# Trading PSUM banks between the gated units and the merge units, turning the last S5 outputs two jobs later, and fetching the residual rows tile by tile in a hybrid decoder trunk

## The chip, the core and the metric

One core of a Trainium2 chip runs the whole program. The metric is the device time of one launch in microseconds (us). The engines are TensorE (PE, matmuls), VectorE (DVE), ScalarE (ACT), GpSimd (POOL) and SyncE (SP, here only DMA issues); each runs its own instruction list in order and waits on semaphores.

## The reference

Two layers over 528 tokens (16 meta tokens and 512) of width 1024. Each layer mixes tokens in two parallel branches and then runs a channel mixer (dense in layer 0, top-2-of-8 experts in layer 1).

```python
z = hn @ w_in[layer]                      # 3584 columns: u_s5, x_lru, g_lru, gates
gates = sigmoid(z[..., o_m:] + merge_bias).reshape(bsz, t, 2, D_MODEL)
# S5 branch: state space model per group, GELU, then a gated unit
y = gelu(y_ssm); y_a = (y * sigmoid(y @ w_glu + b_glu)) @ s5_w_proj
y_b = rglru_branch(...) @ lru_w_proj
y = gates[:, :, 0, :] * y_a + gates[:, :, 1, :] * y_b
hs = hs + y @ w_out[layer]
hn = rmsnorm(hs, ffn_norm[layer])         # then the channel mixer
```

## The kernel before

Activations lie transposed, channels on partitions in tiles of 128, and tokens along the free dimension: `hs`, `hn`, `gates`, `xh` and so on have one row block `[:, m, :]` for each channel tile m. Every fp32 operand of a large product is split into a high and a low part (`xh`, `xl` for activations, `wh`, `wl` for weights), and a product is three matmuls: high by high, high by low, low by high. In layer 0 each runs as two matmuls of 264 tokens, in layer 1 mostly as one of 512.

The weights come in **units** of 8 blocks of 128x128 (512 KB). SP fetches unit u into `raw` when the low part of unit u-3 has been made; ACT makes `wh` (`split_hi`, L740) and DVE `wl` (`split_lo`) two units ahead of PE's use. `unit` (L1724) runs a unit as 8 **jobs**, one for each block, of three products. A dictionary `between` can put other work ahead of job n of a unit.

A mixer has 28 input units k (`U_IN`), 2 gated units (`U_GLU`), 8 merge units and 8 output units. Beside the input units run the S5 steps of 8 batches of groups, in the four `side` banks.

- **Input unit 27** is the last. Ahead of its job 1 stands `turn_last` (L1712): PE transposes the last S5 outputs `ys`, which ACT copied out of PSUM (L849, in `s5_last`). ACT copies the result into `zt` (L852). Ahead of job 4 stands `regroup_last` (L1720), 8 products that place `zt` by channels into `side` banks 2 and 3. ACT applies the GELU to the half that came by DMA (L855) and to this half (L857), and rounds it into `y1h` (L860); DVE makes `y1l`. Only after `s5_last` does ACT run its last step for unit 27, a sigmoid that reads unit 27's sums in `acc` (L904) and frees them.
- **Gated units** g = 0, 1 multiply `y1h`/`y1l` by the GLU weights. `glu_sums` puts g = 0 into both pairs of `acc` banks and g = 1 into the `side` banks. PE waits, ahead of g = 0, until ACT has freed both halves of `acc` (`free(0, a1)`, `free(1, a1)`). ACT takes the sigmoid of the sums (L945).
- **Merge units** m = 0 to 7 compute both branches' projections for channel tile m. `merge_sums` puts even m into `acc`, odd m into `side`. DVE multiplies the sums by `gates[:, m, :]` and `gates[:, 8 + m, :]`, adds, and signals `mg_ready`; ACT rounds to `xh` (L954), and DVE makes `xl`. The gates occupy the memory of `hs` and `hn`, tile by tile.
- After the eight merge steps ACT issues eight DMAs (L957) that bring the residual rows `hs[:, m, :]` back from HBM (from the input `xT` in layer 0, from `hs_d` in layer 1). Then come the square-root table and the next weight splits.
- **Output units** m = 0 to 7 multiply by `w_out`, in `acc[:, m % 2]`. DVE waits for all eight row blocks (`hs_back`) before it adds the first one (L1372); a no-op behind each add frees that half of `acc` (L1375). Output unit 2 needs the half that unit 0 used. From unit 2 on, PE adds sums of squares for the norm (L1750) in `side` bank 0.

## Time and profile before

| what | value |
|---|---|
| three timed runs | 1754.74, 1755.19, 1757.77 us; median 1755.19 |
| span of the profiled execution | 1751.1 us |
| median less span | 4.1 us |
| PE busy | 1646.0 us, 94% |
| DVE, ACT, POOL busy | 58%, 44%, 21% |
| chain that ended last | PE 78%, DVE 7%, issue 5% |

The span runs from the first to the last instruction of one profiled execution; its other overheads lie around it and no time of its own is given beside the span, so the sums of the prediction are made against 1751.1 and the 4.1 us to the median are carried over unchanged. In the rows below a matmul's own duration (0.28 us for 264 columns) is longer than the distance from one to the next, since matmuls overlap.

### The profile page before, as it was taken

Reading aid. Unit: us, or ns where it says so; the run is one execution under the profiler, and the core shown is the slowest. Engines: PE = TensorE matmul, PEld = TensorE weight load, DVE = VectorE, ACT = ScalarE, POOL = GpSimd, SP = SyncE. Lnnn points to the kernel's source line nnn. Section 1 sums busy time; section 2 is a strip of 40 time slices with the busy share of each in tenths; the row PEclk is TensorE's granted clock in tenths of the full one; section 3 lists DMA queues with packets and bytes.
Section 4 is the critical chain, followed back from the end, with each engine's and each line's share of the span. In section 5 each row is a group of like instructions: output and inputs, shape, how many; then the busy total and the mean of one; then the engine's idle time right before and its main releaser. Section 6 shows DMA issues by size and latency. Waiting matters only on the chain.

```text
span 1751.1 us, 26958 instructions
## 1 busy us (share of the span) xinstructions
PE 1646.0 (94%) x10652; PEld 1465.3 (84%) x10652; DVE 1020.8 (58%) x1286; ACT 777.5 (44%) x947; POOL 370.7 (21%) x662
## 2 busy tenths in 40 slices
PE   6899999989999999998999999979999999999992
PEld 5799989989999999998987877757788777777872
DVE  6868567443333233324766766368556766865985
ACT  4354463332221222323453563247536655755772
POOL 7688630020000000004777700020000000000001
PEclk9899999999999999998999999999999999999996
DMA  4523222473232222224523224059658967966994
GB/s 161 118 83 92 77 79 86 146 273 123 85 96 85 87 94 91 89 85 148 119 81 94 73 87 146 25 231 405 242 189 286 358 220 242 384 247 227 368 370 158
DMA packets 99444, 291.24 MB, mean 166 GB/s; under 512 B 27376, under 2 KB 27504, under 8 KB 99200
## 3 DMA queue, kind: packets, MB, share of 16 engines
q1 hardware_dynamic: 84624, 245.43, 41.3%
q0 software_dynamic: 9504, 33.60, 5.4%
q10 hardware_dynamic: 5200, 10.64, 1.8%
q8 instruction: 75, 1.23, 0.3%
q14 instruction: 41, 0.34, 0.1%
HBM read 261.39 MB, written 28.24 MB: 165 GB/s over the span
## 4 chain that ended last, share of the span: by engine, by line
PE 78%; DVE 7%; issue 5%; POOL 4%; DMA 3%; ACT 3%; ACTq 0%; POOLq 0%; DVEq 0%; SPq 0%
PE acc L1740 41%; PE acc L2005 7%; PE acc L2006 7%; PE acc L2007 7%; PE side L1740 3%; PE acc L1783 2%; PE acc L2003 2%; DMA mraw<-in_W 2%; PE acc L2004 2%; DVE rot L1154 1%; POOL pt L533 1%; PE side L1803 1%; PE side L2051 1%; POOL pt L649 1%; PE side L1865 1%
## 5 line engine op out<-in xcount | busy, mean ns | idle before, releaser
L1154 DVE TENSOR_TENSOR mwl<-mraw,mwh 128x1024 fp32r<-128x1024 f32 x288 | 337.7, 1220 | 75.2 <-ACT mwh L1049 74.4
L1740 PE MATMUL acc<-xh,wh 128*128 128x264 f32 (+1 forms) x1584 | 374.9, 306 | 5.0 <-DVE xl L1154 1.8
L1740 PE MATMUL acc<-xl,wh 128*128 128x264 f32 (+1 forms) x1584 | 367.0, 302 | 0.0
L1740 PE MATMUL acc<-xh,wl 128*128 128x264 f32 (+1 forms) x1584 | 366.1, 301 | 0.0
L1154 DVE TENSOR_TENSOR wl<-raw,wh 128x1024 fp32r<-128x1024 f32 x164 | 203.5, 1242 | 212.4 <-ACT wh L740 211.7
L1049 ACT ACTIVATE mwh<-mraw 128x1024 fp32r<-128x1024 f32 x288 | 288.1, 1053 | 61.5 <-PE acc L2007 31.8
L1740 PEld LDWEIGHTS acc<-xh,wh 128*128 128x128 f32 x1584 | 255.5, 189 | 19.8 <-issue 3.3
L1740 PEld LDWEIGHTS acc<-xh,wl 128*128 128x128 f32 x1584 | 253.9, 189 | 9.6
L1740 PEld LDWEIGHTS acc<-xl,wh 128*128 128x128 f32 x1584 | 254.3, 189 | 9.0
L740 ACT ACTIVATE wh<-raw 128x1024 fp32r<-128x1024 f32 x164 | 172.2, 1051 | 143.7 <-PE acc L1740 141.1
L2005 PE MATMUL acc<-mwh,xth 128*128 128x512 f32 x432 | 171.1, 396 | 7.9 <-ACT ytok L1115 5.4
L2007 PE MATMUL acc<-mwl,xth 128*128 128x512 f32 x432 | 169.1, 391 | 0.0
L2006 PE MATMUL acc<-mwh,xtl 128*128 128x512 f32 x432 | 169.1, 391 | 0.0
L697 POOL DMA_DIRECT2D yg_d<-ytok x11 | 6.0, 541 | 524.3 <-ACT ytok L1115 520.7
L2005 PEld LDWEIGHTS acc<-mwh,xth 128*128 128x128 f32 x432 | 81.5, 189 | 27.7 <-DVE mwl L1154 6.7
L2007 PEld LDWEIGHTS acc<-mwl,xth 128*128 128x128 f32 x432 | 81.5, 189 | 17.4
L2006 PEld LDWEIGHTS acc<-mwh,xtl 128*128 128x128 f32 x432 | 81.5, 189 | 16.4
L597 POOL DMA_DIRECT2D gw<-in_wg x2 | 1.1, 546 | 424.7 <-DVE hs L1408 424.7
L2005 PE MATMUL acc<-mwh,hth 128*128 128x512 f32 x216 | 86.0, 398 | 0.0
L2007 PE MATMUL acc<-mwl,hth 128*128 128x512 f32 x216 | 84.2, 390 | 0.0
L2006 PE MATMUL acc<-mwh,htl 128*128 128x512 f32 x216 | 84.2, 390 | 0.0
L1740 PE MATMUL acc<-fh,wh 128*128 128x264 f32 x384 | 78.8, 286 | 0.0
(405 smaller groups left out, 2626.1 us busy)
## 6 DMA issues: line engine op xcount, KB each, us to landing
mraw<-in_W SPq DMA_DIRECT2D x288, 512.0 KB, 5.3
raw<-in_W SPq DMA_DIRECT2D x164, 512.0 KB, 3.5
xg_d<-zero POOLq DMA_DIRECT2D x15, 512.0 KB, 9.9
yg_d<-ytok POOLq DMA_DIRECT2D x9, 512.0 KB, 4.7
xt<-xg_d POOLq DMA_DIRECT2D x8, 512.0 KB, 8.5
pbuf<-in_s5m POOLq DMA_DIRECT2D x16, 192.0 KB, 3.2
yg_d<-zero POOLq DMA_DIRECT2D x5, 512.0 KB, 20.8
hs<-in_xT SPq DMA_DIRECT2D x8, 264.0 KB, 8.1
```

The source lines that it names most:

```text
L533: link(g.tensor_tensor(out, a, b, op))
L649: g.tensor_tensor(z1, phase[:, :, :, 0:n], br, ALU.mult)
L740: a.activation(wh[s][:, :], raw[s][:, :], ACT.Copy).then_inc(hi_ready[s], 1)
L1049: a.activation(mwh[w][:, :], mraw[j % RAWS][:, :], ACT.Copy).then_inc(wide_hi, 1)
L1154: return v.tensor_tensor(out, a, b, op)
L1740: ins = mm(out, w, x[:, t0:t1], start=first and i == 0, stop=last and i == 2)
L1783: ins = mm(acc[:, a, b, 0:TH], w, x[:, b * TH:(b + 1) * TH], start=k == 0 and i == 0, stop=k == DK - 1 and i == 2)
L2003: ins = mm(out[0:HALF], hi[:, 0:HALF], mwl[w][:, cols], start=False, stop=False)
L2004: return ins if first else mm(out, hi, mwh[w][:, cols], start=False, stop=last)
L2005: mm(out, hi, mwh[w][:, cols], start=first, stop=False)
L2006: mm(out, lo, mwh[w][:, cols], start=False, stop=False)
L2007: return mm(out, hi, mwl[w][:, cols], start=False, stop=last)
```

## The change

Four edits, in both layers.

1. The gated unit g = 0 and the even merge units take the `side` banks, the gated unit g = 1 and the odd merge units take `acc`. The semaphores that free the banks are traded with them. Ahead of gated unit 0 PE now waits for the last GELU (`y1_ready`, which ACT's L857 completes, the last reader of `side`), and ahead of gated unit 1 for ACT's sigmoids of units 26 and 27.
2. Output unit 0 writes `side` banks 0 and 1; output units 1 to 7 stay in `acc`.
3. In unit 27 `turn_last` stands ahead of job 3 instead of job 1, and `regroup_last` ahead of job 5 instead of job 4.
4. ACT issues the DMA of residual row block m behind the rounding of merge step m, instead of all eight after step 7.

```diff
         def glu_sums(g, i):
-            return side[:, 2 * i:2 * i + 2, :] if g else acc[:, i, :, :]
+            return acc[:, i, :, :] if g else side[:, 2 * i:2 * i + 2, :]
         def merge_sums(m):
-            return (side[:, 0:2, :], side[:, 2:4, :]) if m % 2 else (acc[:, 0, :, :], acc[:, 1, :, :])
+            return (acc[:, 0, :, :], acc[:, 1, :, :]) if m % 2 else (side[:, 0:2, :], side[:, 2:4, :])
+        def out_sums(m):
+            return acc[:, m % 2, :, :] if m else side[:, 0:2, :]
...
                     a.activation(xh[:, m, AT0[l]:T], ft[:, 0, AT0[l]:T], ACT.Copy).then_inc(xh_ready, 1)
-
-                for m in range(DK):
                     act.dma_start(hs[:, m, :], (hs_d if l else xT)[:, m, :]).then_inc(hs_back, 16)
+
                 sqrt_table()
...
-                    v.tensor_tensor(live(l, hs[:, m, :]), live(l, hs[:, m, :]), summed(l, acc[:, m % 2, :, :]),
+                    v.tensor_tensor(live(l, hs[:, m, :]), live(l, hs[:, m, :]), summed(l, out_sums(m)),
...
-                         between={1: lambda: turn_last(l), 4: lambda: regroup_last(l)} if k == U_IN - 1 else None)
+                         between={3: lambda: turn_last(l), 5: lambda: regroup_last(l)} if k == U_IN - 1 else None)
...
                 for g in range(U_GLU):
                     if g == 0:
+                        pe.wait_ge(y1_ready, (l + 1) * (MT + 1))
+                    else:
                         free(0, a1)
                         free(1, a1)
...
-                        if m % 2 == 0:
+                        if m % 2:
                             free(i, a0 + 15 + m // 2)
                         else:
                             pe.wait_ge(side_free[i], l * SIDE_MIX + 1 + m // 2)
...
                 for m in range(DK):
-                    free(m % 2, a0 + 19 + m // 2)
                     if m == 0:
+                        pe.wait_ge(side_free[0], (l + 1) * SIDE_MIX)
                         pe.wait_ge(xl_ready, xl_mix_end(l) - 1)
+                    else:
+                        free(m % 2, a0 + 19 + m // 2)
```

PE in input unit 27 of layer 0, before. `wh_57` and `wl_60` are the high and low weights of the ring slot of unit 27; three rows are one job. The transposes are L1712, the products that regroup are L1720.

```order
L1740 MATMUL acc<-xh,wl_60 128x264 x2
L1712 MATMUL side<-ident,ys 66x128 x4
L1740 MATMUL acc<-xh,wh_57 128x264 x2
L1740 MATMUL acc<-xl,wh_57 128x264 x2
L1740 MATMUL acc<-xh,wl_60 128x264 x2
L1740 MATMUL acc<-xh,wh_57 128x264 x2
L1740 MATMUL acc<-xl,wh_57 128x264 x2
L1740 MATMUL acc<-xh,wl_60 128x264 x2
L1740 MATMUL acc<-xh,wh_57 128x264 x2
L1740 MATMUL acc<-xl,wh_57 128x264 x2
L1740 MATMUL acc<-xh,wl_60 128x264 x2
L1720 MATMUL side<-ident,zt 64x66 x8
```

The same place after the change, from the end of job 1 on (lines have moved by three).

```order
L1743 MATMUL acc<-xh,wl_60 128x264 x2
L1743 MATMUL acc<-xh,wh_57 128x264 x2
L1743 MATMUL acc<-xl,wh_57 128x264 x2
L1743 MATMUL acc<-xh,wl_60 128x264 x2
L1715 MATMUL side<-ident,ys 66x128 x4
L1743 MATMUL acc<-xh,wh_57 128x264 x2
L1743 MATMUL acc<-xl,wh_57 128x264 x2
L1743 MATMUL acc<-xh,wl_60 128x264 x2
L1743 MATMUL acc<-xh,wh_57 128x264 x2
L1743 MATMUL acc<-xl,wh_57 128x264 x2
L1743 MATMUL acc<-xh,wl_60 128x264 x2
L1723 MATMUL side<-ident,zt 64x66 x8
```

Three jobs stand ahead of the transposes instead of one, two jobs between them and the regrouping instead of three, and three jobs behind it instead of four.

ACT at the end of the merge in layer 0, before: the steps for merge units 5, 6 and 7 and the way to output unit 0.

```order
L954 ACTIVATE xh<-ft 128x528
L740 ACTIVATE wh_59<-raw_56 128x1024
L954 ACTIVATE xh<-ft 128x528
L740 ACTIVATE wh_57<-raw_54 128x1024
L954 ACTIVATE xh<-ft 128x528
L957 DMA hs<-in_xT 128x528 x8
L755 ACT_TABLE_LOAD
L755 ACTIVATE warm<-ones 128x1
L740 ACTIVATE wh_58<-raw_55 128x1024
```

The same stretch of ACT after the change.

```order
L958 ACTIVATE xh<-ft 128x528
L959 DMA hs<-in_xT 128x528
L744 ACTIVATE wh_59<-raw_56 128x1024
L958 ACTIVATE xh<-ft 128x528
L959 DMA hs<-in_xT 128x528
L744 ACTIVATE wh_57<-raw_54 128x1024
L958 ACTIVATE xh<-ft 128x528
L959 DMA hs<-in_xT 128x528
L759 ACT_TABLE_LOAD
L759 ACTIVATE warm<-ones 128x1
L744 ACTIVATE wh_58<-raw_55 128x1024
```

Each merge step has one of the eight issues behind its rounding, and one is left ahead of the table load.

## Rows read from the trace of the kernel before

**Rows 1.** The page: shares of the chain that ended last, by engine.

```profile
PE 78%; DVE 7%; issue 5%; POOL 4%; DMA 3%; ACT 3%; ACTq 0%; POOLq 0%; DVEq 0%; SPq 0%
```

**Rows 2.** Chain of waits, layer 0, unit 27 and gated units: start, us, what.

```profile
243.98 0.29 ACT ys L849
...
244.94 2.19 PE acc L1740 x18
247.13 1.08 PE side L1720 x16
248.21 3.12 PE acc L1740 x24
251.32 1.81 issue
253.13 6.08 PE acc L1740 x48
259.22 5.84 PE side L1740 x48
```

**Rows 3.** Timeline of PE in unit 27, layer 0 (start, us, operation, idle before).

```profile
242.40 0.40 PE L1740 MATMUL acc<-xh,wl 128*128 128x264 f32 x2
244.31 0.63 PE L1712 MATMUL side<-ident,ys 128*66 128x128 f32 x4 [1.51 <-ACT ys L849]
```

**Rows 4.** Timeline of ACT beside it.

```profile
244.98 0.59 ACT L852 ACTIVATE zt<-side 66x512 f32<-66x512 f32 x1 [0.72 <-PE side L1712]
...
246.88 0.64 ACT L855 ACTIVATE yt<-yt 64x528 f32<-64x528 f32 x1
248.25 0.61 ACT L857 ACTIVATE yt<-side 64x528 f32<-64x528 f32 x1 [0.72 <-PE side L1720]
...
252.33 0.70 ACT L904 ACTIVATE gates<-acc,cols 128x528 f32<-128x528 f32 x1
```

**Rows 5.** Timeline of DVE beside it: low parts of gated unit 0's weights, last tile.

```profile
242.00 1.23 DVE L1154 TENSOR_TENSOR wl<-raw,wh 128x1024 fp32r<-128x1024 f32 x1 [2.02 <-ACT wh L740]
...
250.10 1.17 DVE L1154 TENSOR_TENSOR y1l<-yt,y1h 128x528 fp32r<-128x528 f32 x1 [3.75 <-ACT y1h L860]
```

**Rows 6.** Chain of waits, layer 1, the same place.

```profile
1016.51 0.29 ACT ys L849
...
1016.84 0.63 PE side L1712 x4
...
1020.65 2.97 PE acc L1740 x12
1023.62 1.92 issue
...
1031.33 5.56 PE side L1740 x24
```

**Rows 7.** Timeline of PE in layer 1: last matmul of unit 27's job 0.

```profile
1015.43 0.40 PE L1740 MATMUL acc<-xh,wl 128*128 128x512 f32 x1
```

**Rows 8.** Timeline of ACT's DMA issues, layer 0, after merge step 7.

```profile
314.23 0.65 ACT L954 ACTIVATE xh<-ft 128x528 fp32r<-128x528 f32 x1 [4.28 <-DVE ft L1154]
314.24 3.84 ACTq L957 DMA_DIRECT2D hs<-in_xT  x8
```

**Rows 9.** Chain of waits, layer 0, output units 0 to 2.

```profile
317.50 5.51 DMA hs<-in_xT
...
323.11 0.72 DVE hs L1372
```

**Rows 10.** Timeline of PE, first matmuls of output unit 2, layer 0.

```profile
323.93 0.51 PE L1740 MATMUL acc<-xh,wh 128*128 128x264 f32 x2 [0.16 <-DVEq L1375]
```

**Rows 11.** Timeline of PE, layer 1: end of output unit 1, start of unit 2.

```profile
1092.13 0.39 PE L1740 MATMUL acc<-xh,wl 128*128 128x512 f32 x1
1094.08 0.50 PE L1740 MATMUL acc<-xh,wh 128*128 128x512 f32 x1 [1.56 <-DVEq L1375]
```

**Rows 12.** The row fetches of L957 (both layers), by line.

```profile
DMA to landing us min/median/max: 2.8/4.2/6.4
```

**Rows 13.** The weight fetches of L491, by line, whole program.

```profile
DMA to landing us min/median/max: 3.3/3.5/9.3
```

**Rows 14.** Windows: engines' busy us, then PEclk, DMA share, GB/s at the end.

```profile
251.20:253.13 1.93, 0.12 (x2) 0.03 (x1) 1.20 (x2) 1.92 (x3) 0.00 (x0) 1.00 0.00 0
...
324.00:375.00 51.00, 46.34 (x387) 43.72 (x388) 22.56 (x28) 15.01 (x22) 11.48 (x21) 0.93 0.44 148
```

More of the change, by code:

```diff
@@ L945, in mixer @@
                         a.activation(live(l, gt[:, i, :]), summed(l, glu_sums(v, i)), ACT.Sigmoid,
-                                     bias=col("b_glu", l, 2 * v + i)).then_inc((side_free if v else acc_free)[i], 1)
+                                     bias=col("b_glu", l, 2 * v + i)).then_inc((acc_free if v else side_free)[i], 1)
                     for i in range(2):
@@ L1337, in mixer @@
                         m = 2 * g + i
-                        dve.wait_ge(*((side_free[i], l * SIDE_MIX + 1) if g else (acc_free[i], a1 + 1)))
+                        dve.wait_ge(*((acc_free[i], a1 + 1) if g else (side_free[i], l * SIDE_MIX + 1)))
                         if m >= 2:
@@ L1357, in mixer @@
                         dve.wait_ge(xl_ready, xh_at_mix(l) + m)
-                    freed, n = (side_free, l * SIDE_MIX + 1) if m % 2 else (acc_free, a0 + 15)
+                    freed, n = (acc_free, a0 + 15) if m % 2 else (side_free, l * SIDE_MIX + 1)
                     for i in range(2):
@@ L1892, in mixer @@
                 for m in range(DK):
-                    free(m % 2, a0 + 19 + m // 2)
                     if m == 0:
+                        pe.wait_ge(side_free[0], (l + 1) * SIDE_MIX)
                         pe.wait_ge(xl_ready, xl_mix_end(l) - 1)
+                    else:
+                        free(m % 2, a0 + 19 + m // 2)
                     unit(u0 + U_MIX - DK + m,
-                         [(k, m % 2, xh[:, k, :], xl[:, k, :], k == 0, k == DK - 1) for k in range(DK)],
-                         before={DK - 1: (xl_ready, xl_mix_end(l))} if m == 0 else None, short=l)
+                         [(k, 0, xh[:, k, :], xl[:, k, :], k == 0, k == DK - 1) for k in range(DK)],
+                         before={DK - 1: (xl_ready, xl_mix_end(l))} if m == 0 else None, short=l, sums=(out_sums(m),))
                     if m >= 2:
```

## The prediction

> **What bounds the kernel now.** I read the page first, then the chain of waits, then the timelines of PE, ACT and DVE around the places that the change touches. PE holds 78% of the chain that ended last [rows 1], so a microsecond in which PE stands still in a mixer is a microsecond of the whole, unless something later takes it back. The questions are therefore where PE stands still around input unit 27 and the output units, and what would hold it next.
>
> There are three such stops that the edits touch, each met once in each layer.
>
> First, ahead of the transposes of the last S5 outputs PE sits idle for 1.51 us, released by ACT's copy of `ys` [rows 3]. That copy ends at 243.98 + 0.29 = 244.27 [rows 2], whatever PE does in the meantime, because ACT is working through other things; only one job of unit 27 is behind PE by then.
>
> Second, after the last matmul of unit 27 the chain shows 1.81 us of "issue" and gated unit 0 starts at 253.13 [rows 2]. The profile gives this wait no releaser, but one fits: ACT's sigmoid of unit 27 runs from 252.33 for 0.70 us, to 253.03 [rows 4], and it is what frees the half of `acc` that gated unit 0 overwrites. ACT runs it so late because the whole S5 tail (zt, two GELUs, `y1h`) stands ahead of it in ACT's list. The operands of gated unit 0 were there: its low weights by 243.23 and the last `y1l` by 251.27 [rows 5].
>
> Third, output unit 2 waits for the half of `acc` that DVE frees when it has added unit 0, and DVE waits for all eight residual row blocks. In layer 0 the chain goes through a row fetch of 5.51 us and the add at 323.11 [rows 9] and PE idles only 0.16 us [rows 10]; in layer 1 it idles 1.56 us [rows 11].
>
> **The turn moved by two jobs, and gated unit 0 in the side banks.** These have to be summed together, since they share one stretch. A unit of 48 matmuls takes 5.84 us in steady state, a job 0.73 us [rows 2]. In layer 0 job 0 ends at 242.40 + 0.24 = 242.64 [rows 3]. After the change jobs 1 and 2 follow at once, to 244.11. `ys` is there at 244.27 and the transposes start at 244.31 as before: the same time, with two jobs more behind PE. Jobs 3 and 4 run until about 244.94 - 0.24 + 0.08 + 1.46 = 246.24 (the chain counts the last transposes in full, PE resumes some 0.24 before their end, and a change of shape costs 0.08). The regrouping can start at 246.3; `zt` is ready at 244.98 + 0.59 = 245.57 [rows 4], 0.7 us earlier, so two jobs in between are enough. It takes 1.08 us [rows 2]. The last three jobs take 2.2 us and a restart of 0.1, so unit 27 ends at 249.7. It ended at 248.21 + 3.12 = 251.3 less the overlap, 251.2 [rows 2]: 1.5 us earlier, which is two jobs of 0.73.
>
> Gated unit 0 then no longer asks for the sigmoid of unit 27, but for the last GELU. The regrouping is done at 247.4, the first half's GELU at 246.88 + 0.64 = 247.52, so the second runs from 247.5 for 0.61 us, to 248.1 [rows 4]. Even at its old place it would end at 248.86. Unit 27 ends at 249.7, so the new wait has 1.6 us to spare and costs nothing. What is queued behind this wait on PE are only the gated units. The last `y1l`, 0.7 us earlier than before, comes at 250.6 [rows 5] and is needed by job 6 of gated unit 0, at 249.7 + 4.4 = 254.1. The sigmoid of unit 27 is now needed only by gated unit 1, at 249.7 + 5.9 = 255.6; ACT ends it at 252.3 (0.7 us earlier than 253.03). Its cover is 3.3 us; gone, it would be paid one for one. Gated unit 0 starts at 249.7 instead of 253.13: **3.4 us** in layer 0.
>
> In layer 1 a job takes 5.56 / 8 = 0.695 us [rows 6]. Job 0 ends at 1015.66 [rows 7], jobs 1 and 2 at 1017.05, which is 0.25 us later than `ys` (1016.80) [rows 6]; the turn starts at 1017.1 rather than 1016.84. Resuming at 1017.5, two jobs (1.4 + 0.1), the regrouping at 1019.1 (1.08) and three jobs (2.1 + 0.1) put the end of unit 27 at 1022.35. It was 1020.65 + 2.97 = 1023.62, and gated unit 0 began 1.92 us later, at 1025.54 [rows 6]: **3.2 us**.
>
> **The other banks.** The merge units' alternation is turned round as a whole. Each merge unit still writes banks that were read one unit earlier, so the distance stays one unit of 5.84 us; DVE and ACT read from `side` what they read from `acc`, and chain rows give the two the same unit time. Merge unit 0 waits on `side`, freed by sigmoids that are over a whole unit before. Output unit 0 in `side` waits for merge 6's products instead of writing `acc` behind the same products: nothing. Its squares (L1750) go into bank 0 only after DVE's add. I take zero for all of this.
>
> **Residual rows inside the merge.** Eight issues take ACT 3.84 us, 0.48 each [rows 8]. Seven of them move into stretches in which ACT waits 4.28 us for DVE's next sum [rows 8], so they cost ACT nothing on the way; each can hold the next weight split back by up to 0.48 us, and that split serves a unit two units ahead. Behind the rounding of step 7 one issue is left, so the last block is on its way at about 314.6 + 0.45 = 315.1 and lands 2.8 to 6.4 us later [rows 12], at 317.9 to 321.5, where before it was 323.0. The square-root table and the next weight splits come 3.4 us earlier too. Without its stop output unit 2 would start at 323.93 - 0.32 = 323.6 [rows 10], so unit 0 ends one unit earlier, near 317.8, and DVE's add ends between 318.7 and 322.3, before PE asks for it at 323.6. The stop goes: 0.16 us idle and 0.16 of overlap in layer 0 [rows 10], in layer 1 1094.08 - 1092.13 - 0.23 = 1.72 us [rows 11]. In layer 1, with units of 5.56 us, the margin of 1.3 us at the longest landing is some 0.6 us smaller and still positive, so nothing is late next. Sum **2.0 us**.
>
> Total: 3.4 + 3.2 + 2.0 = **8.6 us**. Span 1751.1 - 8.6 = 1742.5; with the 4.1 us around it, **1746.6 us**, 0.49% less. No operation is added or removed, so no other term is needed; what comes behind each mixer starts from PE's or DVE's last step and moves with it as a block.
>
> **The clock, as row and as rule.** In the stop of 1.9 us ahead of gated unit 0 the granted clock stays at 1.00, the 2.4 GHz level [rows 14]. Removing the stop therefore brings nothing on top of its own length. At the end of the mixer of layer 0, where PE idles through the norm, the stretch 324 to 375 has a mean of 0.93 [rows 14]: 0.07 x 51 / 0.5 = 7.1 us at the lower level, 1.2 GHz. The Trainium skill's page "TensorE: Matmul & The Clock Gate", section "Part 1: The HAM clock gate", says that the monitor runs freely and does not reset with the kernel, so where it switches relative to the work depends on phase. By that rule the same joint could lose more or less after a shift; no row here can show it, and it is a rival below.
>
> **Rivals.**
>
> *The joints fall otherwise on the clock.* The change moves everything after layer 0's unit 27 by 3 to 9 us. If the low-clock stretch of 7.1 us is longer or shorter by its half at one joint, 3.6 us of it at half speed are 1.8 us; at two joints in the same direction 3.6. That gives 1743.0 to 1750.2. For it: the three timed runs differ by 3.0 us with nothing changed. Against: a median evens some of it out.
>
> *Only the output part works.* If gated unit 0 still started when it does now, because what ended the 1.81 us was not the sigmoid but something that the profile does not show ("issue" names none), only the 2.0 us and perhaps the two jobs per layer would be saved: if the new stop swallowed the jobs too, 1753.2; that is within 0.2%. Against it stands that the sigmoid's end, 253.03, and PE's start, 253.13, fit to 0.1 us.
>
> *Row fetches in the way of the weights (slower).* Row blocks of 264 KB now travel among weight units of 512 KB. A weight unit is fetched about three units of 5.84 us ahead of its split, some 15 us after ACT's and DVE's own work is taken off, and lands in 3.5 us, 9.3 at the worst [rows 13]. If the rows slowed it beyond 15 us, each of 8 merge units in 2 layers would be late by the excess; at an excess of 1 us that is 16 us less the 8.6, so 1762.6. The decisive point is a landing of 15 us, four times the median. Against: at the end of the merge, where eight row blocks are issued in a row, a row block still lands in at most 6.4 us [rows 12]. The Trainium skill's page "Trainium Kernel Development and Optimization", section "Key Constraints", says that DMAs of all queues share the same 16 engines and interleave, so that a second queue saves only issue time; that is the mechanism, and by it alone 0.78 MB in 5.84 us instead of 0.52 would stretch landings but no total.
>
> **How the numbers follow.** Forecast (7.5 to 9.5 us saved) 0.60; the clock rival (5 to 12 us saved, 0.27; of this about one tenth lies beyond the ends of my range); only a part (0 to 4 us saved) 0.08; slower 0.05. A measurement of this kernel can tell a difference of about 0.2%, 3.5 us, from none: the bound is 1751.7. Faster by more: 0.60 + 0.27 = 0.87. Within: 0.08. Slower: 0.05. The range from 1743.0 to 1751.0 holds the forecast and most of the clock rival and leaves out the last two.
>
> **What the new profile would show.** The transposes of the last outputs start within 0.3 us of their old time after `ys`, with idle of 0.3 us or less in place of 1.51; the products that regroup follow two jobs later without idle; gated unit 0 starts right behind unit 27, about 5.4 us after the transposes in place of 8.8; ACT's sigmoid of unit 27 now runs while gated unit 0 does. Output unit 2 follows unit 1 without a wait on DVE's no-op in both layers, and the landing of the row fetches in the merge is near 3 us. Wrong would be: a wait for the GELU or for `zt` on PE, a longer wait for `wh` or `wl` anywhere in the merge, or a saving that is given back at the norms with a clock of 0.5 for longer than now.

## The result and the profile after

| | before | after |
|---|---|---|
| median (lowest to highest), 4 runs each | 1754.97 us (1753.12 to 1757.77) | 1742.48 us (1739.56 to 1743.21) |
| ratio, 95% interval | | 0.9925 (0.9913 to 0.9936) |
| profiled execution: span | 1751.1 us | 1740.4 us |
| its device time | not known | 1742.03 us |
| mean granted clock in it | 0.979 | 0.977 |

The change saves 12.5 us by the medians, 0.71%; the ratio in the table says 0.75%. The forecast was 8.6 us and 1746.6 us, with a range of 1743.0 to 1751.0: the direction is right, and the time lies 0.5 us below the range. The two profiled spans differ by 10.7 us.

PE in unit 27 and gated unit 0 of layer 0, timeline of after (start, us, operation; an idle time before it would stand in brackets at the end):

```profile
243.78 0.40 PE L1743 MATMUL acc<-xh,wl 128*128 128x264 f32 x2
244.21 0.63 PE L1715 MATMUL side<-ident,ys 128*66 128x128 f32 x4
244.60 0.49 PE L1743 MATMUL acc<-xh,wh 128*128 128x264 f32 x2
...
246.22 1.15 PE L1723 MATMUL side<-ident,zt 66*64 66x66 f32 x16
...
249.36 0.40 PE L1743 MATMUL acc<-xh,wl 128*128 128x264 f32 x2
249.60 0.41 PE L1743 MATMUL side<-y1h,wh 128*128 128x264 f32 x2
```

The idle of 1.51 us ahead of the transposes [rows 3] is gone: jobs 1 and 2 run in it. Gated unit 0 starts at 249.60, 0.24 us behind the last product of unit 27, where it started at 253.13 behind 1.81 us of "issue" [rows 2]. What stood in its way is seen on ACT, timeline of after:

```profile
244.88 0.59 ACT L856 ACTIVATE zt<-side 66x512 f32<-66x512 f32 x1 [0.72 <-PE side L1715]
245.49 1.28 ACT L859 ACT_TABLE_LOAD   x1
...
247.45 0.61 ACT L861 ACTIVATE yt<-side 64x528 f32<-64x528 f32 x1
248.09 1.19 ACT L864 ACTIVATE y1h<-yt 128x528 fp32r<-128x528 f32 x1
...
251.55 0.70 ACT L908 ACTIVATE gates<-acc,cols 128x528 f32<-128x528 f32 x1
...
255.64 1.29 ACT L949 ACTIVATE gt<-side,cols 128x528 f32<-128x528 f32 x2 [2.44 <-PE side L1743]
```

The sigmoid of unit 27 (L908) runs from 251.55, while gated unit 0 is under way: it was 252.33 before [rows 4]. The last GELU (L861), for which PE now waits, is over at 248.06, 1.5 us ahead of the unit that needs it.

Layer 1, the chain of waits of after (start, us, what, merged matmuls):

```profile
1011.49 2.14 PE acc L1743 x9
1013.63 0.44 PE side L1715 x4
1014.07 1.40 PE acc L1743 x6
1015.47 1.08 PE side L1723 x16
1016.54 2.28 PE acc L1743 x9
1018.82 5.58 PE side L1743 x24
...
1080.02 11.12 PE acc L1743 x48
1091.14 0.35 PE side L1753 x8
```

Every piece follows the one before; the 1.92 us of "issue" [rows 6] is gone. So is the stop ahead of output unit 2: units 1 and 2 are one piece of 48 matmuls, 11.12 us, which is twice 5.56 (1.56 us idle stood between them [rows 11]). The landing of the row fetches that did it, by the line that issues them, and one of DVE's adds in layer 0:

```profile
L959 ACTq DMA_DIRECT2D hs<-in_xT x8: 334/334/339, 269.5 to 310.6; - x8
...
DMA to landing us min/median/max: 2.6/2.7/3.4
```

```profile
314.90 0.70 DVE L1375 TENSOR_TENSOR hs<-hs,side 128x528 f32<-128x528 f32 x1
```

Issued singly, a row block lands in 2.7 us (4.2 before, 6.4 at the most [rows 12]), and DVE adds unit 0 right behind its split of the next weights, without a wait for the rows (the add of before started at 323.11 [rows 9]).

### The profile page after: what moved, and what is told of

The parts are those of the page before. It is cut to its first block and busy times, and to the rows that moved or that the text cites. A ratio compares the mean times of both kernels' runs of the same rounds, so it can differ in the third digit from the quotient of the medians.

```text
span 1740.4 us, 26958 instructions
## 1 busy us (share of the span) xinstructions
PE 1645.2 (95%) x10652; PEld 1466.3 (84%) x10652; DVE 1021.3 (59%) x1286; ACT 778.3 (45%) x947; POOL 371.8 (21%) x662
## 5 line engine op out<-in xcount | busy, mean ns | idle before, releaser
L1743 PE MATMUL acc<-xh,wh 128*128 128x264 f32 (+1 forms) x1560 | 368.1, 306 | 3.4 <-DVE xl L1157 1.8
L1743 PE MATMUL acc<-xl,wh 128*128 128x264 f32 (+1 forms) x1560 | 360.3, 301 | 0.0
L1743 PE MATMUL acc<-xh,wl 128*128 128x264 f32 (+1 forms) x1560 | 359.3, 300 | 0.0
L1743 PEld LDWEIGHTS acc<-xh,wh 128*128 128x128 f32 x1560 | 251.2, 189 | 17.2 <-issue 3.3
L1743 PEld LDWEIGHTS acc<-xl,wh 128*128 128x128 f32 x1560 | 250.2, 189 | 8.7
L1743 PEld LDWEIGHTS acc<-xh,wl 128*128 128x128 f32 x1560 | 249.7, 189 | 9.3
```

Source lines behind the costliest of these rows:

```text
L1743: ins = mm(out, w, x[:, t0:t1], start=first and i == 0, stop=last and i == 2)
```

## The experiments

All times stand against runs of the kernel before on the same chip. Clock means are over all runs of a kernel. One table is used for several of them: DVE does the same instructions in the same order in every kernel here, so that the start of one and the same DVE instruction can be compared. It gives the change of a stretch's length against the profile of before, in us, worked out from the traces and good to 0.1 us; the stretches are named by their times in before. "Low" is where the granted clock is 0.5 (start in us of its own trace). One profile is one execution: it need not lie at the median of its kernel (e3 and e9 were slow ones).

```
stretch         0-240  240-262  262-357  357-1005  1005-1034  1034-1124  1124-end    sum   low in 240-262, 1005-1124
holds                  turn,    output             turn,      output
                       gated 0  unit 2             gated 0    unit 2
before            0       0        0         0         0          0         0         0    none
e15_before_again +0.3    0.0     +0.3      +0.4      +1.5       +0.6      -1.6      +1.5   1028
e16_before_third +0.3    0.0     +0.2      +0.5      +1.6       +0.3      -0.8      +2.1   1028
after            -0.1   -3.5     -0.6      +0.6      -3.3       -1.9      -1.8     -10.6   none
e4_again         +0.1   -3.5     -0.5      -2.1      -3.3       -1.9      -1.0     -12.2   none
e1_banks         +0.2   -2.1     +0.3      -1.2      -2.2       +0.7      -1.7      -6.0   none
e2_turn          -0.3   +0.8     +0.3      -0.8      -0.5       +0.2      -1.7      -2.0   252
e12_no_turn      -0.6   -2.0     -0.6      -0.9      -2.1       -1.9      -0.3      -8.4   none
e11_no_rows      -0.1   -3.5      0.0      +0.4      -3.4       +2.5      +0.4      -3.7   1089
e5_fill          -0.2    0.0     +0.3       0.0      -0.1       +2.1      +1.0      +3.1   1095
e13_fill_out     +0.2    0.0     +1.1      -0.4      +1.5       +0.8      +0.5      +3.7   1028
e14_fill_gated   +0.1    0.0     +0.4      -0.5       0.0       +2.0      -1.1      +0.9   1095
e3_rows          +1.9    0.0     -0.6      +0.6      +1.6       -1.8      -1.0      +0.8   1029
e8_hold          +1.7   +2.1     -0.5      -1.8      -0.3       -1.8      -0.7      -1.4   254
e9_fill_stops    +1.0    0.0     +0.2      +0.6       0.0       +1.6      -1.0      +2.4   none
```

### The three parts alone

**e1_banks**: the banks traded (edits 1 and 2 of the change), the turn at jobs 1 and 4, the rows after the merge.

```diff
-                         between={3: lambda: turn_last(l), 5: lambda: regroup_last(l)} if k == U_IN - 1 else None)
+                         between={1: lambda: turn_last(l), 4: lambda: regroup_last(l)} if k == U_IN - 1 else None)
...
-                    act.dma_start(hs[:, m, :], (hs_d if l else xT)[:, m, :]).then_inc(hs_back, 16)
-
+
+                for m in range(DK):
+                    act.dma_start(hs[:, m, :], (hs_d if l else xT)[:, m, :]).then_inc(hs_back, 16)
                 sqrt_table()
```

(The diff is against after.)

> Only the banks are traded; the turn stays ahead of job 1 and the rows are fetched after the merge. Theory (each edit takes away its own stop of PE, nothing else): gated unit 0 starts at the end of unit 27, 251.2 in the timing of before instead of 253.1, and in layer 1 2.1 us earlier, so 4.0 us less; the wait of 1.5 and 1.0 us for ys and the stop ahead of output unit 2 (1.6 us idle in layer 1) stay. Rival (the sigmoid of unit 27 is not what gated unit 0 waited for): it starts as late as before, 0 us. Rival (the clock gives more than the stops): over 6 us less, with low-clock stretches shorter than in the kernel before.

Measured: 1746.65 us against 1754.72, 8.1 less, ratio 0.9961 (0.9948 to 0.9973). In its trace gated unit 0 follows unit 27 at once, the idle of the turn stays at 1.47 and 1.02 us, and output unit 2 still waits. The table gives 2.1 and 2.2 us for the two gated stops. The ratio is worth 6.8 us (4.7 to 9.1), more than the 4.0 that the theory had, and that is the first sign that a stop costs more than its length, or that the profile of before was a short one.

**e2_turn**: edit 3 alone.

```diff
-                         between={1: lambda: turn_last(l), 4: lambda: regroup_last(l)} if k == U_IN - 1 else None)
+                         between={3: lambda: turn_last(l), 5: lambda: regroup_last(l)} if k == U_IN - 1 else None)
```

> Only the turn and the regrouping are moved. Theory: unit 27 ends 1.5 us earlier in layer 0, but gated unit 0 still waits for the sigmoid of unit 27, which ACT can start only some 0.7 us earlier (0.3 in layer 1), so 1.1 us less in all, and the idle of PE ahead of gated unit 0 grows from 1.8 to some 2.6 us. Rival (the turn is worth its two jobs by itself): 2.6 us less. Rival (a longer stop lets the clock fall): a stretch at 0.5 behind it and a time that is longer than before.

Measured: 1753.80 against 1754.72, ratio 0.9998 (0.9989 to 1.0006): no gain that the runs can tell, though the interval also holds the 1.1 us of the theory. Timeline of PE at gated unit 0 in this kernel, and the windows around it (us, busy us of PE, PEld, DVE, ACT, POOL, then PEclk, DMA share, GB/s):

```profile
249.13 0.41 PE L1740 MATMUL acc<-xh,wl 128*128 128x264 f32 x2
252.12 0.78 PE L1740 MATMUL acc<-y1h,wh 128*128 128x264 f32 x2 [2.58 <-issue]
252.70 0.64 PE L1740 MATMUL acc<-y1l,wh 128*128 128x264 f32 x2
```

```profile
248.00:252.00 4.00, 1.54 (x13) 1.32 (x11) 2.27 (x2) 3.97 (x5) 0.00 (x0) 1.00 0.00 0
252.00:256.00 4.00, 3.88 (x19) 3.91 (x20) 1.23 (x1) 0.97 (x2) 0.00 (x0) 0.57 0.59 154
```

Unit 27 ends 1.5 us earlier, but gated unit 0 still waits for the sigmoid, so the stop swallows most of the gain: 1.81 us have become 2.58. And here, other than in [rows 14], the clock does fall after the stop: 0.57 over four us, and a product takes 0.64 us instead of 0.40, as the third rival had it. In layer 1 the stop is as long, 2.71 us, and the clock stays up (the table has one low stretch, at 252).

**e3_rows**: edit 4 alone, in the kernel before.

```diff
                     a.activation(xh[:, m, AT0[l]:T], ft[:, 0, AT0[l]:T], ACT.Copy).then_inc(xh_ready, 1)
-
-                for m in range(DK):
                     act.dma_start(hs[:, m, :], (hs_d if l else xT)[:, m, :]).then_inc(hs_back, 16)
+
                 sqrt_table()
```

> Only the residual rows are fetched inside the merge. Theory: the stop ahead of output unit 2 goes in both layers; with the restart of the matmul pipeline that each stop costs beside its idle time, 0.65 us in layer 0 and 1.9 us in layer 1, 2.6 us in all. Rival (rows slow the weights): waits for wh or wl in the merge, and no gain. Rival (clock): a gain that differs from 2.6 us by more than 2.

Measured: 1750.56 against 1754.72, 4.2 less, ratio 0.9981 (0.9971 to 0.9990), where the term of the sum was 2.0. The ratio is worth 3.3 us (1.8 to 5.1), which holds the 2.6 of the theory and, just, the 2.0; that the term was too small is read from the traces below. Both stops of output unit 2 are gone. The clock fell after the gated stop of layer 1:

```profile
1027.56 0.47 PE L1739 MATMUL acc<-y1h,wh 128*128 128x512 f32 x1 [1.91 <-issue]
```

```profile
1028.00:1034.00 6.00, 6.00 (x21) 4.76 (x20) 1.23 (x1) 0.41 (x1) 0.00 (x0) 0.72 0.51 178
```

The first line is of PE's timeline, the second the window behind it, with a clock of 0.72 over six us: 0.28 x 6 / 0.5 = 3.4 us at the lower level.

### One part taken out of the change

**e11_no_rows**: after, with the eight row fetches behind the merge again. **e12_no_turn**: after, with the turn at jobs 1 and 4.

```diff
-                    act.dma_start(hs[:, m, :], (hs_d if l else xT)[:, m, :]).then_inc(hs_back, 16)
-
+
+                for m in range(DK):
+                    act.dma_start(hs[:, m, :], (hs_d if l else xT)[:, m, :]).then_inc(hs_back, 16)
                 sqrt_table()
```

> The changed kernel with the rows fetched after the merge again. Theory: the stop ahead of output unit 2 comes back, at the size of the traces of the other runs (0.5 us idle in layer 0, 2.0 in layer 1, with restarts 0.9 and 2.4), 3.3 us, and 0 to 1.5 us for the clock: 1744.5 to 1747 us. Rival (the size in the trace of before, 2.0 us without restarts as in the prediction): 1743.5 us.

> The changed kernel with the turn ahead of job 1 and the regrouping ahead of job 4 again. Theory: unit 27 ends 1.5 us later in layer 0 and 1.1 us in layer 1, with a restart each of 0.3 us hidden in it, and nothing behind hides it, so 2.6 to 3.2 us over the changed kernel, against the 1.1 us that the same edit brought alone; 1744 to 1745.5 us. Rival (the turn is worth 1 us here as well): 1743 us.

Measured: e11 1747.15 against 1754.12, ratio 0.9960 (0.9946 to 0.9975), 7.0 us less, where after and e4 have 12.5 and 13.6, so 5.5 to 6.6 above after; e12 1745.55, ratio 0.9948 (0.9935 to 0.9961), by the same count 4 to 5 us above. Both lie at the upper end of what was expected or just beyond it. With the banks traded, the moved turn is worth its two jobs in each layer: in the table 3.5 less 2.0 and 3.3 less 2.1 us, 2.7 in all; where the other 1 to 2 us of e12 come from is not shown. Alone (e2) it brought nothing that the runs can tell. In e11 the stop of layer 1 is longer than in the profile of before, and the clock fell behind it:

```profile
1088.42 0.69 PE L1744 MATMUL acc<-xh,wh 128*128 128x512 f32 x1 [2.46 <-DVEq L1379]
```

```profile
1088.00:1092.00 4.00, 3.58 (x9) 2.80 (x10) 3.35 (x4) 2.21 (x3) 0.00 (x0) 0.57 0.29 77
```

**e8_hold**: after, but gated unit 0 waits for the two sigmoids too, as it did before, so that only the wait comes back.

```diff
                     if g == 0:
                         pe.wait_ge(y1_ready, (l + 1) * (MT + 1))
-                    else:
-                        free(0, a1)
-                        free(1, a1)
+                    free(0, a1)
+                    free(1, a1)
```

> The changed kernel, but gated unit 0 again waits for ACT's sigmoids of units 26 and 27, which it does not need. This gives back the stop and nothing else. Theory: the stops return as 2.65 us in layer 0 and 2.7 us in layer 1, plus 0.3 us for each restart, 5.9 us; and since they are longer than the 1.8 us of before, the clock falls behind them in most executions, up to 1.7 us each, so 6 to 9.3 us over the changed kernel. Rival (clock plays no part): 5.4 to 5.9 us.

Measured: 1750.41 against 1754.75, ratio 0.9973 (0.9963 to 0.9984), 8 to 9 us above after. That settles the 1.81 us of "issue" of [rows 2]: it is the sigmoid. The stops in its trace are 2.69 and 2.82 us, and with a restart of some 0.3 us each they come to 6.1. By the table the two stretches are 5.6 and 3.0 us longer than in after: the whole of the rest is in layer 0. Behind the stop of layer 1, the longer one, the clock stays up (1.00 over 1026 to 1032); behind that of layer 0 it is at the lower level for 6.8 us:

```profile
254.28 0.78 PE L1743 MATMUL side<-y1h,wh 128*128 128x264 f32 x2 [2.69 <-issue]
```

```profile
252.00:256.00 4.00, 1.72 (x8) 1.75 (x9) 2.36 (x3) 2.98 (x4) 0.00 (x0) 0.70 0.27 101
256.00:260.00 4.00, 4.00 (x20) 4.00 (x20) 0.27 (x1) 0.00 (x0) 0.00 (x0) 0.50 0.46 165
260.00:262.00 2.00, 2.00 (x17) 2.00 (x17) 0.00 (x0) 0.00 (x0) 0.00 (x0) 0.89 0.00 0
```

**e4_again**: after, unchanged, as the measure for the others.

> The changed kernel once more, beside the same runs of the kernel before. Theory: 9.3 us from the stops (4.1 in layer 0, 5.2 in layer 1), the rest of the 12.5 us measured is where the clock fell in the executions, so the difference of medians is between 8 and 13 us and each execution's time goes with its mean granted clock: about 3.5 us for 0.002. Rival (the stops themselves are worth 12 us, since the profile understates them): 12 to 13 us again, and no relation to the clock.

Measured: 1741.17 us (1738.56 to 1742.90) against 1754.72, 13.6 less, ratio 0.9925 (0.9912 to 0.9938), at and beyond the upper end of the 8 to 13 us of the theory. Its other half held: of the nine runs of the changed kernel (with those of the first result) the five at a mean clock of 0.977 took 1741.88 to 1743.21 us and the four at 0.979 took 1738.56 to 1741.17, about 2.7 us less.

### Is it the clock? Stops filled with products

Here PE multiplies constants into `side` banks that are free at that time; nobody reads the results, so all that is computed is added work. The filler stands ahead of a wait:

```diff
+            def fill(out, n):
+                for _ in range(n):
+                    mm(out, ident[:, :], ones[:, :], start=True, stop=True)
...
                     if g == 0:
+                        fill(side[:, 0, 0:P], 6)
                         free(0, a1)
                         free(1, a1)
```

**e5_fill** is this diff on the kernel before. **e14_fill_gated** has 8 in place of 6. **e13_fill_out** has none there, but 7 ahead of the wait of output unit 2 in layer 1. **e9_fill_stops** puts fillers into all three kinds of stop: 6 ahead of gated unit 0, 5 and 3 ahead of the transposes (layers 0 and 1), 5 ahead of output unit 2 in layer 1.

> The kernel before, with six extra products of two constants (128x128x128, fp32, results never read) ahead of gated unit 0 in each layer, in the time in which PE would stand still. The stop stays as long as it was. Theory (in part of its executions the kernel before loses the fast clock at that stop, 1.7 us each time; the profiled one happened not to): the median falls by 1 to 3.5 us with gated unit 0 starting no earlier relative to the turn, and no low-clock stretch follows it. Rival (the clock at the stops plays no part, the missing 4 us of the prediction come from elsewhere): the median stays within 0.5 us of before, or rises by what the fillers are too long.

> The kernel before with fillers in all three stops of both layers (turn, gated unit 0, output unit 2) and nowhere else, so the stops stay and PE is kept busy in them. Theory (each stop is a chance for the clock to fall, and five of them cost the kernel before 2 to 3 us that the changed kernel doesn't pay): mean clock 0.978 to 0.980 instead of 0.977, and 1 to 3 us less than before. Rival (the earlier run with fillers at gated unit 0 alone found no gain because the clock at the stops plays no part; the difference of the clock lies at the joints by phase): within 1 us of before and the same mean clock.

> The kernel before with 7 filler products (14 matmuls, some 1.75 us, results unused) in layer 1 ahead of the wait for the bank of output unit 2, nothing else. Theory (in the executions in which the clock falls after this stop, the fall costs 1.7 us; it fell in 2 of the 5 profiles that have the stop without fillers, after idle of 2.03 and 2.46 us): 2/5 x 1.7 = 0.7 us less than before on average, and the profile shows no low clock within 10 us behind the stop. Rival (a fall there only takes the place of one elsewhere, so the sum of the low clock stays): the mean granted clock stays at 0.977 and the time within 0.3 us of before, or up to 0.3 us more where the fillers run past the release.

> The kernel before with 8 filler products (16 matmuls, some 2.0 us) ahead of gated unit 0 in both layers, two more than in the earlier kernel with 6, so that of its idle of 0.48 and 0.58 us nothing or 0.1 us is left. Theory (the clock fell after this stop in 3 of 8 cases, two layers of four profiles with the stop open, and a fall costs 1.7 us): 2 x 3/8 x 1.7 = 1.3 us less than before, mean granted clock up by 0.0007. Rival (what the kernel with 6 fillers showed, 1.4 us more at an unchanged clock, is how it is: a stop filled here gives nothing): 1754 to 1757 us with the clock at 0.976 to 0.977.

| kernel | us | before, same chip | ratio (interval) | mean clock (before) |
|---|---|---|---|---|
| e5_fill | 1756.15 | 1754.75 | 1.0004 (0.9994 to 1.0015) | 0.9762 (0.9770) |
| e14_fill_gated | 1755.92 | 1754.41 | 1.0006 (0.9995 to 1.0017) | 0.9773 (0.9768) |
| e13_fill_out | 1755.01 | 1754.41 | 1.0003 (0.9992 to 1.0014) | 0.9769 (0.9768) |
| e9_fill_stops | 1752.81 | 1754.12 | 0.9988 (0.9980 to 0.9997) | 0.9792 (0.9765) |

To fill one kind of stop gives no gain that the runs can tell. The expectations of e5 and e14 by my theory missed, and their rivals held; the interval of e13 holds both its theory (0.7 us less) and none. The traces show falls elsewhere. In e14 the gated stops are filled to the end:

```profile
251.25 1.95 PE L1710 MATMUL side<-ones,ident 128*128 128x128 f32 x16
253.22 0.48 PE L1744 MATMUL acc<-y1h,wh 128*128 128x264 f32 x2
```

and then the clock falls behind the other stop of layer 1, ahead of output unit 2:

```profile
1094.52 0.50 PE L1744 MATMUL acc<-xh,wh 128*128 128x512 f32 x1 [2.03 <-DVEq L1375]
```

```profile
1094.00:1100.00 6.00, 5.48 (x17) 4.37 (x18) 3.45 (x4) 2.21 (x3) 0.00 (x0) 0.72 0.46 127
```

e5 shows the same fall, at 1095. e13, with that stop filled, shows it at 1028, behind the gated stop. In the stretch from 1005 to 1124 one fall was seen in each of the three, at the stop that was left, and none in e9, which alone gains, 1.3 us. But the fillers of e9 did not close the stops. They are over at 1095.49, and ahead of output unit 2 PE is then idle for as long as in e5 and e14, since the last row block took 7.96 us to land. No fall follows:

```profile
1097.52 0.50 PE L1745 MATMUL acc<-xh,wh 128*128 128x512 f32 x1 [2.03 <-DVEq L1375]
```

```profile
1094.00:1100.00 6.00, 3.97 (x23) 3.31 (x22) 2.99 (x4) 2.17 (x3) 0.00 (x0) 1.00 0.47 122
```

So an idle time of 2.03 us brings a fall in two kernels and none in a third. These are single profiles, and the counts are small.

### The base: the kernel before, profiled again

The edit of **e15_before_again** and **e16_before_third** is none.

> The kernel before, unchanged, for a second profile of it. Theory (the profile that I predicted from was a fast execution, with short stops ahead of output unit 2): the span is 1752.5 to 1754.5 us instead of 1751.1, the idle ahead of output unit 2 is 0.4 us or more in layer 0 and 1.7 us or more in layer 1 (0.16 and 1.56 there), and the clock falls in one of the mixers in about half of such profiles. Rival (the profile was typical, and only something outside the span differed): the span is 1751 +- 0.5 us, and the stops are 0.2 and 1.6 us.

> The kernel before once more, unchanged, for a third profile, since the landing of the row fetches differs from one execution to the next. Theory: as for the second, stops ahead of output unit 2 of 0.4 us or more and 1.7 us or more, span 1752.5 to 1754.5 us. Rival: 0.2 and 1.6 us, span 1751 us.

Measured: 1754.11 and 1754.69 us, spans 1752.6 and 1753.2. The theory held, and the clock fell in both where about half was expected. The stop of layer 0 is 0.63 and 0.52 us (0.16 in the profile that I predicted from), that of layer 1 2.15 and 1.84 (1.56), and the fall is in layer 1. In e15, timeline of PE, first gated unit 0, then output unit 2:

```profile
1026.49 0.47 PE L1740 MATMUL acc<-y1h,wh 128*128 128x512 f32 x1 [1.91 <-issue]
```

```profile
1097.19 0.51 PE L1740 MATMUL acc<-xh,wh 128*128 128x512 f32 x1 [2.15 <-DVEq L1375]
```

The landing of the last row block is what makes the difference. In the chain of waits of e15:

```profile
1089.41 6.89 DMA hs<-hs_d
1096.30 0.03 issue
```

against 6.37 us in the profile of before. In e16 the clock over the stretch behind the gated stop is 0.72, in e15 0.73; that of e16:

```profile
1028.00:1034.00 6.00, 6.00 (x20) 4.72 (x20) 0.70 (x1) 0.01 (x1) 0.00 (x0) 0.72 0.40 132
```

So the profile of before was a short execution, and so say the times: of the 86 runs of the kernel before in the four comparisons, 11 took 1752.7 us or less, which is its span of 1751.1 plus the 1.5 to 1.6 us by which the device time exceeds the span in every run that has both.

### Both kernels with fillers in the long stops, and a faster version

**e6_warm_after** is after with fillers ahead of the long waits of the whole program: the first S5 batch, some of the LRU's rotations, the norms, the router, the experts' start. **e7_warm_before** is the kernel before with the same and with the fillers of e9. The norms' part, as an example of the edit:

```diff
                 add_squares(2 * l + 1, DK - 2)
+                fill(side[:, 1, 0:P], 3)
                 add_squares(2 * l + 1, DK - 1)
+                if l == 0:
+                    fill(side[:, 1, 0:P], 4)
...
                 spread_inverse(i)
+                fill(side[:, 1, 0:P], 8)
```

> The changed kernel, with such fillers in every longer idle stretch of PE: at the first S5 batches, at the norms between the stages, in the router, and ahead of the first expert. The fillers are counted to be no longer than the idle time that the trace shows. Theory: the low-clock stretches of the changed kernel (38 us in which PE is busy at half speed, outside the tail) mostly go; where PE alone is the limit each gives back half, so 8 to 17 us less than the changed kernel, 1725 to 1733 us, and the executions lie closer together. Rival (the stretches are hidden behind DVE and DMA anyway): less than 4 us. Rival (fillers run late): the waits behind them grow and the time rises.

> The kernel before with the same fillers, and with fillers in the three stops that the change removes. Theory: with the clock kept up in both, the two kernels differ by the stops alone, 9.3 us (4.1 in layer 0, 5.2 in layer 1) or up to 0.6 less for restarts that the fillers hide, so 8.5 to 9.5 us over the changed kernel with fillers. Rival (the change is worth its 12 to 13.5 us through the stops alone): 12 us or more. Rival (prediction's sum, no restarts): 8.6 us; this and the theory can be told apart only by the traces.

Measured: e6 1732.62 us (1732.08 to 1733.42), ratio 0.9874 (0.9857 to 0.9891); e7 1742.89 us (1742.50 to 1745.65), ratio 0.9935 (0.9921 to 0.9949). The first lines of e6's page:

```profile
span 1730.6 us, 27418 instructions
...
PE 1655.5 (96%) x10882; PEld 1476.8 (85%) x10882; DVE 1022.2 (59%) x1286; ACT 778.6 (45%) x947; POOL 374.1 (22%) x662
...
PEclk9999999999999999999999999999999999999996
```

230 more matmuls, all of them useless, make the program 8.6 to 10 us shorter than e4 and after: the mean clock goes from 0.978 to 0.990. With the clock kept up in both kernels (0.990 each) the change is worth 10.3 us, between the 8.5 to 9.5 of the theory and the 12 of its rival. (In e7 idle times of 0.4 to 0.6 us are left at the turns and the gated stops, and 1.47 us ahead of output unit 2 of layer 1.) e6 is 22 us below the kernel before and the fastest kernel of this study.

**e10_warm2**: e6, with the 10 fillers of the first S5 batch ahead of another wait, one step earlier.

```diff
+                        if n == 0:
+                            fill(side[:, 3, 0:P], 10)
                         pe.wait_ge(m_act, n + 1)
                         pe.wait_ge(m_dve, n + 1)
...
-                        if n == 0:
-                            fill(side[:, 0, 0:P], 10)
                         pe.wait_ge(u_in if b > 1 else u_in0, 16 * L * (l + 1))
```

> The changed kernel with fillers as in e6_warm_after, but at the first S5 batch they stand ahead of the wait for DVE's m3 instead of behind it, where they delayed the next products by 3.9 us. Theory: the low-clock stretch at 60 us goes too (1.7 us) and the delay of about 1 us behind it, so 1 to 3 us less than e6_warm_after: 1730 to 1731.5 us, the fastest of all. Rival (the S5 chain of DVE sets the time there): within 0.5 us of e6_warm_after.

Measured: 1733.78 us, 1.2 above e6, where 1 to 3 us less were expected. The low stretch at 60 us went as the theory had it (1.00 over 58 to 66), and a longer one came. The fillers run from 67.65, PE then idles 2.37 us at the next wait, and the clock falls there, where in e6 the fillers stood at 70.88 in that idle time. First e6, then e10:

```profile
70.88 2.84 PE L1713 MATMUL side<-ones,ident 128*128 128x128 f32 x24
```

```profile
72.86 0.62 PE L1877 MATMUL side<-uu,m 128*128 128x66 f32 x2 [2.37 <-DVE state L1157]
```

```profile
72.00:80.00 8.00, 7.14 (x34) 7.14 (x35) 6.82 (x11) 1.34 (x2) 7.38 (x16) 0.57 0.25 68
```

## Why the prediction was right in kind and short in size

The time came 4.1 us below the forecast of 1746.6. Two steps failed. The sum was made against one execution, and the 4.1 us by which the median of before stood above its span were carried over unchanged, where 1.6 us belong around a span: 2.5 us. And the gain was set equal to the lengths of the stops in that execution: the restart behind a stop (0.5 us for the output units) and the clock were put at nothing. What follows goes through the terms.

**Turn and gated unit, 3.4 and 3.2 us: right.** The table has 3.5 and 3.3 us against the profile that the sum was made from. Gated unit 0 was to start at 249.7 and started at 249.60; `ys` and the transposes came where they were expected, and the GELU left 1.5 us to spare instead of 1.6. The releaser that the profile did not name was the sigmoid, as its end at 253.03 against PE's start at 253.13 had said; e8 shows it by putting the wait back, and e2 by the stop that grows when only the turn is moved. The further 0.1 us in each layer is less than what two profiles of one kernel differ by.

**The other banks: nothing, right.** No wait of PE on a merge or output bank appears in after.

**Residual rows, 2.0 us: the mechanism right, the term too small.** The last block was to land at 317.9 to 321.5; its issue, put at 314.6 to 315.1 on the times of before, starts at 310.62, beside the rounding and not behind it and with everything else some 3.6 us earlier, and it lands in 3.4 us at the most, by 314.0, well before PE asks for the bank at about 320. But the stops were sized from one profile. Against that profile the table has 0.6 and 1.9 us, 2.5 in all: the sum left out that PE also needs some 0.25 to 0.3 us to get going again behind a stop (output unit 2 took 5.84 us behind its stop in layer 1 of before, 5.56 without one; [rows 2] had 6.08 us for gated unit 0 behind its stop against 5.84 for the next). Against e15 and e16, and with e4 beside after, it is 0.8 and 2.35, so 3.15 us: the stops there are 0.63 and 0.52 us in layer 0, 2.15 and 1.84 in layer 1. The landing of the eighth of eight fetches issued in a row varies, 5.5 to 6.9 us in the three profiles of the kernel before, and PE pays each tenth of it; singly issued fetches land in 2.5 to 3.5 over all profiles that have them. [rows 12] gave the spread of landings, 2.8 to 6.4, and I used it for the kernel after, not for the stop that goes.

**"Removing the stop brings nothing on top of its own length": wrong.** This step read a clock of 1.00 behind one stop in one execution [rows 14] as a property of the stop. In layer 1 of two of three profiles of the same kernel the clock falls behind the gated stop, to 1.2 GHz for 3.4 us, which is 1.7 us of work lost; the stretch 1005 to 1034 is 1.5 and 1.6 us longer in them. Over all profiles with such a stop left open and unfilled it fell behind the gated one in 2 of 7 (layer 0) and 4 of 7 (layer 1), behind that of output unit 2 in layer 1 in 3 of 8. Length does not decide it within this range: stops of 2.71 and 2.82 us in layer 1 (e2, e8) had no fall behind them, stops of 1.9 us had. Of the five profiles in which both stops of layer 1 are gone (after, e4, e12, e6, e10) none has low clock between 1005 and 1124:

```profile
1005.00:1124.00 119.00, 117.09 (x575) 92.52 (x575) 63.90 (x80) 47.64 (x62) 2.39 (x6) 1.00 0.31 94
```

(Windows of after; PEclk is the 1.00 near the end.) The Trainium skill's page "TensorE: Matmul & The Clock Gate", section "Part 1: The HAM clock gate", says that where the clock switches relative to the work varies from run to run of one kernel. The three profiles of before bear that out: 1.00 over 1028 to 1034 in one, 0.73 and 0.72 in the others. The prediction cited this rule for the norms and not for the stop itself, where it spoke against reading a single row.

The runs say how much the clock can be worth in all. The mean granted clock is 0.97685 over the 86 runs of before and 0.97789 over the nine of the changed kernel. By an estimate from these means that is 0.00104 x 1750 / 0.5 = 3.6 us less at the lower level, and half of it, 1.8 us, less time: about one fall. The spread of the nine runs makes this uncertain by a third or more.

**The 4.1 us around the span: wrong.** Device time less span is 1.5 to 1.6 us in every run that has both. The other 2.5 us were the difference between a short execution and the median, together with the spread of the medians themselves (1754.1 to 1755.2). With 1.6 around it, the profile of before stood for 1752.7 us, and 8.6 less would have been 1744.1; carrying the difference over unchanged meant that the runs' longer stops and their clock falls would stay, though they hung on what the change removes.

**The sum again.** Mean of after and e4 against mean of e15 and e16, from the table: turn and gated unit 3.5 in layer 0 and 3.3 in layer 1; output units 0.8 and 2.35; the fall at 1028 that after does not have 1.55. That is 11.5 us, and 13.2 with what the rest differs by (1.7, mostly in 357 to 1005, where after and e4 differ from each other by 2.7). That difference goes with the clock: the low stretches in 357 to 1005 come to 27.2 us in after, e15 and e16 and to 20.4 in e4, and after is there no faster than e15 and e16 (+0.6 against +0.4 and +0.5). The medians give 12.5 and 13.6. With the clock kept up (e6 and e7) it is 10.3: the stops without the falls.

**The rivals.** The clock rival was the right one to name and was put at the wrong place. It was told of the joints at the norms, which could as well lose as gain, and given 1743.0 at best; at the removed stops it can only gain. The row fetches did not get in the way of the weights: those issued in the merge of layer 0 land in 3.4 to 4.0 us in after, 3.4 to 3.7 before, in layer 1 in 3.3 to 4.2 in both. The case in which only the output part works is refuted by the start of gated unit 0 in after and by e8.

**What stays open.** What decides whether the clock falls behind a stop is not shown. That the fall goes to the stop that is left when another is filled rests on one profile each of e5, e13 and e14, and e9 has such a stop without a fall. A fall also moves all that follows by 1.5 to 1.6 us (e15, e16), so two stops of one layer are not independent. So the 1.55 us belong to the stops together, and no share of them to one stop. Whether the change has a part in the 1.7 us elsewhere is not shown; in 357 to 1005 they come from e4 alone.

## What to carry to other kernels

Before a sum is made against one profiled execution, ask whether it was a typical one: here its device time less its span was taken for overhead, and most of it was that execution's luck in DMA landings and clock. A stop of PE of 1.8 us or more is worth its length, a restart of 0.3 us, and now and then 1.7 us of clock behind it; it brought no gain that could be measured to move work out of its way from one side (e2) or to fill it alone (e5, e13, e14) while its neighbours stayed. Where a wait is hidden behind a bank, trading banks between the unit that comes early and the one that comes late can take the whole stop away, and here it cost nothing (e1).

## What the runs showed of the hardware that I had not expected

- The clock falls behind a stop of 1.9 us in some executions of the same program and not in others (1.00 against 0.73 and 0.72 over 1028 to 1034), and idle times of 2.03, 2.71 and 2.82 us had none behind them in e9, e2 and e8.
- Products that nobody needs, put into PE's long waits, take the mean granted clock from 0.978 to 0.990 and 8.6 to 10 us off the time; put one step too early (e10) they leave an idle time of 2.37 us, and it falls there (0.57 over 72 to 80, 1.00 in e6).
- Eight row fetches of 264 KB issued in a row by ACT land in 2.6 to 8.0 us over the profiles of this study, the same fetches issued one per merge unit in 2.5 to 3.5, although weight fetches of 512 KB run beside them.
- PE's first unit behind a stop is 0.25 to 0.3 us longer than one that follows another.
